# Second block's attention: sliding units mixed with selected ones, heads paired across key groups, block-diagonal compressed keys and values

## The reference

```
qn = rope(kvh(q_n, NSA_HEADS), t).reshape(B, S, NSA_KV, NSA_GROUP, HEAD_DIM)
k_c, k_s, k_w = (rope(kvh(z, NSA_KV), t) for z in (k_c, k_s, k_w))
ckv = jax.vmap(compress)(jnp.stack([k_c, v_c]), cmp_pos, cmp_w1, cmp_w2)   # 31 compressed blocks
o_cmp, p_cmp = compressed_attention(qn, ckv[0], ckv[1], t)
o_slc = selected_attention(qn, k_s, v_s, idx, t)       # 8 blocks of 64, all 8 are chosen: causal
o_win = banded_attention(qn, k_w, v_w, NSA_WINDOW, None)                   # window 512: causal
o_nsa = gates[..., 0:1] * o_cmp + gates[..., 1:2] * o_slc + gates[..., 2:3] * o_win
o_nsa = rms_norm(o_nsa.reshape(B, S, NSA_HEADS * HEAD_DIM), nsa_out_norm)
qw = rope(kvh(q_w, SWA_HEADS), t).reshape(B, S, SWA_KV, SWA_GROUP, HEAD_DIM)
o_swa = banded_attention(qw, kw, kvh(v_sw, SWA_KV), SWA_WINDOW, swa_sinks)  # window 128, with sinks
o_swa = rms_norm(o_swa.reshape(B, S, SWA_HEADS * HEAD_DIM), swa_out_norm)
h = h + rms_norm(jnp.concatenate([o_nsa, o_swa], axis=-1) @ w_out, attn_post_norm)
```

## Time and profile before

| | |
|---|---|
| median of 3 runs | 1889.32 us (1887.1 to 1889.44) |
| the profiled execution | 1890.05 us, its span 1888.2 us |
| TensorE busy | 1825.2 us (97%) |
| VectorE busy | 1332.4 us (71%) |
| ScalarE busy | 975.0 us (52%) |
| GpSimd busy | 190.9 us (10%) |
| HBM traffic | 81 GB/s over the span |

### The profile page before, as it was taken

The page is one execution under the profiler, slowest core; times in us unless marked ns, Lnnn a source line. Parts: engine busy times, 40 slices in busy tenths (PEclk is TensorE's granted clock), DMA queues, the critical chain, the costliest instruction groups (busy, mean ns, idle before and its releaser), DMA issues.

```text
span 1888.2 us, 26991 instructions
## 1 busy us (share of the span) xinstructions
PE 1825.2 (97%) x8975; PEld 1451.8 (77%) x8975; DVE 1332.4 (71%) x1885; ACT 975.0 (52%) x1550; POOL 190.9 (10%) x135
## 2 busy tenths in 40 slices
PE   6999999999999998999999999999898999999998
PEld 5775788888888875688888888887556678888887
DVE  6989777777655899867777755687675567777544
ACT  5468764444433458764444433576665554444322
POOL 0100120000133200020000033200021300000111
PEclk9999999999999999999999999999999999999999
DMA  6220233333233420133333233442000223332332
GB/s 168 71 80 1 65 92 100 93 96 97 77 99 99 109 73 23 33 91 99 90 100 100 72 97 99 109 143 79 12 1 12 78 78 100 91 98 86 89 95 76
DMA packets 285096, 154.46 MB, mean 82 GB/s; under 512 B 16949, under 2 KB 283095, under 8 KB 285015
## 3 DMA queue, kind: packets, MB, share of 16 engines
q1 hardware_dynamic: 284596, 153.26, 28.2%
q10 hardware_dynamic: 419, 0.17, 0.0%
HBM read 151.31 MB, written 2.10 MB: 81 GB/s over the span
## 4 chain that ended last, share of the span: by engine, by line
PE 79%; DVE 9%; issue 6%; ACT 6%; DMA 0%; DVEq 0%; SPq 0%; ACTq 0%
PE bank L575 24%; PE bank L576 24%; PE bank L577 24%; DVE cacc L1770 3%; PE bank L1019 1%; DVE nmax L1837 1%; PE bank L975 1%; PE bank L996 1%; ACT pr L1544 1%; DVE nmax L2071 1%; DVE w_lo L1630 1%; ACT w_hi L1177 1%; ACT pt L1560 1%; DMA x_in<-in_x 0%; PE bank L1091 0%
## 5 line engine op out<-in xcount | busy, mean ns | idle before, releaser
L575 PE MATMUL bank<-h_hi,w_hi 128*128 128x512 f32 x1448 | 571.7, 395 | 6.9 <-DVE w_lo L1630 6.7
L576 PE MATMUL bank<-h_lo,w_hi 128*128 128x512 f32 x1448 | 565.6, 391 | 0.0
L577 PE MATMUL bank<-h_hi,w_lo 128*128 128x512 f32 x1448 | 565.2, 390 | 0.0
L1177 ACT ACTIVATE w_hi<-raw 128x1024 fp32r<-128x1024 f32 (+3 forms) x314 | 312.0, 1000 | 488.2 <-PE bank L577 484.0
L1630 DVE TENSOR_TENSOR w_lo<-raw,w_hi 128x1024 fp32r<-128x1024 f32 (+3 forms) x314 | 375.4, 1201 | 230.9 <-ACT w_hi L1177 230.2
L575 PEld LDWEIGHTS bank<-h_hi,w_hi 128*128 128x128 f32 x1448 | 273.2, 189 | 69.7 <-issue 7.6
L576 PEld LDWEIGHTS bank<-h_lo,w_hi 128*128 128x128 f32 x1448 | 273.4, 189 | 57.8 <-issue 2.2
L577 PEld LDWEIGHTS bank<-h_hi,w_lo 128*128 128x128 f32 x1448 | 273.1, 189 | 57.3
L575 PE MATMUL bank<-a_hi,w_hi 128*128 128x512 f32 x528 | 206.1, 390 | 0.0
L577 PE MATMUL bank<-a_hi,w_lo 128*128 128x512 f32 x528 | 205.5, 389 | 0.0
L576 PE MATMUL bank<-a_lo,w_hi 128*128 128x512 f32 x528 | 205.4, 389 | 0.0
(11 more groups left out here) (317 smaller groups left out, 2258.4 us busy)
## 6 DMA issues: line engine op xcount, KB each, us to landing
raw<-in_w_up SPq DMA_DIRECT2D x132, 512.0 KB, 3.8
raw<-in_w_in SPq DMA_DIRECT2D x39, 512.0 KB, 4.0
raw<-in_w_down SPq DMA_DIRECT2D x48, 384.0 KB, 3.2
raw<-in_w_down SPq DMA_DIRECT2D x48, 320.0 KB, 3.0
raw<-in_w_o SPq DMA_DIRECT2D x16, 512.0 KB, 3.5
raw<-in_cmp_w SPq DMA_DIRECT2D x8, 512.0 KB, 3.9
raw<-in_w_out SPq DMA_DIRECT2D x8, 512.0 KB, 3.4
raw<-in_w_uq SPq DMA_DIRECT2D x8, 288.0 KB, 3.0
```

Of the source, the lines that this page charges most:

```text
L575: mm(o, wh, mh, start=start, stop=False)
L576: mm(o, wh, ml, start=False, stop=False)
L577: return mm(o, wl, mh, start=False, stop=stop)
L1177: last = A_(dst(w_hi), src(raw), ACT.Copy)
```

## The change

1. **Heads.** Pair c is now heads c and c+4, so that its two halves of the partitions belong to the two key groups. `k2` holds each key once (128 partitions x 512), and the rope's sum of ks, kw and kx is one addition of 128 partitions. The q slabs come in two DMAs of 64 columns each (256-byte runs), the output projection's slabs in two DMAs of 64 partitions; ScalarE's split waits for the second by semaphores of its own. Gates, sinks and norm gains are indexed to match.
2. **Compressed branch.** The 31 blocks are padded to 32, and `kcT` and `vcn` become block-diagonal over the two key groups (zeroed by VectorE ahead of the block; two copies each in place of one). `cmp_scores` makes 16 products of 128 rows and 64 columns, `cmp_turned` 4 groups of 4 turns of 64 columns, in k = 3 to 6 of slab t12, ScalarE 4 copies in place of 8. A windowed unit has one product of 64 rows and 128 columns for the compressed branch, in place of two of 31 rows and 64 columns.
3. **Order of the units.** After two NSA units the sliding units alternate with those of NSA pairs 0 and 1 (unit 2 is sliding, unit 3 selected, and so on), then come the last two sliding units; pairs 2 and 3 follow as before. All sliding chunks and the last windowed one gather in bank 7, the others in bank 6; a chunk's first values wait for the eviction of the chunk ahead in its bank. `yw` has a place of its own, 8 KB behind `ct_all`. The sink column is written only where the bank's unit before wasn't of the same sliding chunk: for 5 units in place of 8. The first sliding unit may start when its own query is roped.

```diff
-    [("qn", j, j * P) for j in range(4)] + [("qx", j, 1304 + j * P) for j in range(4)]
+    [("qn", j, j * HD2) for j in range(4)] + [("qx", j, 1304 + j * HD2) for j in range(4)]
...
-UNITS = nsa_units(0) + nsa_units(1) + [(SC_SWA, c, t) for c in range(PAIRS) for t in range(NT)] + nsa_units(2) + nsa_units(3)
-CHUNKS = [(SC_WIN, 0), (SC_WIN, 1)] + [(SC_SWA, c) for c in range(PAIRS)] + [(SC_WIN, 2), (SC_WIN, 3)]
+def mixed_units(lead):
+
+    nsa, swa = nsa_units(0) + nsa_units(1), [(SC_SWA, c, t) for c in range(PAIRS) for t in range(NT)]
+    pairs = [unit for both in zip(swa, nsa[lead:]) for unit in both]
+    return nsa[:lead] + pairs + swa[len(nsa) - lead:]
+
+
+UNITS = mixed_units(2) + nsa_units(2) + nsa_units(3)
+CHUNKS = [(b, c) for b, c, t in UNITS if t == NT - 1 and b != SC_SLC]
+O_BANK = {chunk: 7 if chunk[0] == SC_SWA or chunk == (SC_WIN, 3) else 6 for chunk in CHUNKS}
...
+def banked_ahead(u):
+
+    mine = chunk_of(u)
+    was = [chunk_of(n) for n in range(u) if O_BANK[chunk_of(n)] == O_BANK[mine] and chunk_of(n) != mine]
+    return [CHUNKS.index(was[-1]) + 1] if was else []
...
+def sink_new(u):
+
+    return UNITS[u][0] == SC_SWA and (u < 2 or UNITS[u - 2][:2] != UNITS[u][:2])
...
-                    c = T_ORDER[i][2]
-                    load(G2, p, slot(p, KD, P), d_in2[:, :, c:c + P])
+                    name, _, c = T_ORDER[i]
+                    if name[0] != "q":
+                        load(G2, p, slot(p, KD, P), d_in2[:, :, c:c + P])
+                        continue
+                    load(G2, p, slot(p, KD, P)[:, :, 0:HD2], d_in2[:, :, c:c + HD2])
+                    sp.dma_start(slot(p, KD, P)[:, :, HD2:P], d_in2[:, :, c + PAIRS * HD2:c + (PAIRS + 1) * HD2])\
+                        .then_inc(q2_ready[i - (len(T_ORDER) - 2 * PAIRS)], 16)
...
-                load(G2, S2_O + n, slot(S2_O + n, PAIRS, 2 * P), d_out2[:, k0:k0 + PAIRS, j * 2 * P:(j + 1) * 2 * P])
+                to = slot(S2_O + n, PAIRS, 2 * P)
+                of = A["w_out_2"][0].rearrange("(z e c p) n -> z e p c n", z=2, e=2, c=PAIRS)[k0 // PAIRS]
+                load(G2, S2_O + n, to[0:HD2, :, :], of[0, :, :, j * 2 * P:(j + 1) * 2 * P])
+                sp.dma_start(to[HD2:P, :, :], of[1, :, :, j * 2 * P:(j + 1) * 2 * P]).then_inc(o2_ready[n], 16)
...
                 for t in range(NT):
                     for c in range(PAIRS):
-                        for e in range(2):
-                            v0 = c // (PAIRS // KV2) * NC
-                            last = mm(C_B[e][:, (t * PAIRS + c) * NC:(t * PAIRS + c + 1) * NC], qn[half(e), c, t * P:(t + 1) * P],
-                                      kcT[half(e), v0:v0 + NC], start=True, stop=True)
...
+                        o = (t % 2 * PAIRS + c) * 2 * NCP
+                        last = mm(C_B[t // 2][:, o:o + 2 * NCP], qn[:, c, t * P:(t + 1) * P], kcT[:, :], start=True, stop=True)
...
             def turn_between(k):
-                for n in ((), (0,), (1,), (2,), (3,), (4,), (5,), (6, 7))[k]:
-                    cmp_turned(n)
+                if 3 <= k < 3 + NT:
+                    cmp_turned(k - 3)
...
-                    if b == SC_SWA and t < 2:
-                        last = mm(o[e][:, 2 * P:2 * P + 1], eye, sinks[:, 2 * c + e:2 * c + e + 1], start=True, stop=True)
+                    if sink_new(u):
+                        last = mm(o[e][:, 2 * P:2 * P + 1], eye, sinks[:, c + PAIRS * e:c + PAIRS * e + 1], start=True, stop=True)
...
-                if i == 1 and t == 0:
-                    pe.wait_ge(sw_done.sem, len(ROPED))
-                if t == 0 and i >= 2 and b != SC_WIN:
-                    pe.wait_ge(y_done.sem, y_done.at(N, i - 1))
-                    if i == 7:
+                if t == 0 and b != SC_WIN:
+                    if chunk_of(u) == (SC_SWA, 0):
+                        pe.wait_ge(sw_done.sem, len(ROPED))
+                    for n_ahead in banked_ahead(u):
+                        pe.wait_ge(y_done.sem, y_done.at(N, n_ahead))
+                    if chunk_of(u) == (SC_WIN, 3):
                         pe.wait_ge(rstd_done.sem, rstd_done.at(N, 3))
...
                 if b == SC_WIN:
-                    for e in range(2):
-                        last = mm(o[half(e), tok], vcn[0:NC, vc0:vc0 + HD2], ct_all[0:NC, c, t, e, :], start=False, stop=True)
+                    last = mm(o[:, tok], vcn[0:2 * NCP, :], ct_all[0:2 * NCP, t, c, :], start=False, stop=True)
...
                 else:
-                    outs = [(k2[kind][o * 64:(o + 1) * 64, hd, :], slice(hd * 64, (hd + 1) * 64))
-                            for hd in range(KV2) for o in range(2)]
-                for o, part in outs:
-                    last = v.tensor_tensor(o, tz[part, 2, :], tz[part, 3, :], ALU.add)
-                last.then_inc(rope_done.sem, 1)
+                    out = k2[kind][:, :]
+                v.tensor_tensor(out, tz[:, 2, :], tz[:, 3, :], ALU.add).then_inc(rope_done.sem, 1)
...
+            v.memset(kcT[:, :], 0.0).then_inc(flat_done.sem, 1)
+            v.memset(vcn[:, :], 0.0).then_inc(flat_done.sem, 1)
```

More of the change, by code:

```diff
@@ L394, in build @@
         vg_ready = [sem(f"vg_ready{i}") for i in range(NV)]
+        q2_ready = [sem(f"q2_ready{i}") for i in range(2 * PAIRS)]
+        o2_ready = [sem(f"o2_ready{i}") for i in range(KD)]
+        flat_done = tally("flat_done")
         xe_f, xe_h, xe_l = tally("xe_f"), tally("xe_h"), tally("xe_l")
@@ L886, in cmp_turn @@
                 for m in range(2):
-                    last = nc.tensor.transpose(bank[6 + t][:, m * 64:m * 64 + 2 * NC], hidc[0:2 * NC, t, m * P:(m + 1) * P],
-                                               const[0:2 * NC, K_EYE:K_EYE + 2 * NC])
+                    last = nc.tensor.transpose(bank[6 + t][:, m * 2 * NCP:(m + 1) * 2 * NCP], hidc[0:2 * NCP, t, m * P:(m + 1) * P],
+                                               const[0:2 * NCP, K_EYE:K_EYE + 2 * NCP])
                 last.then_inc(hid_t.sem, 1)
@@ L894, in cmp_keys @@
                 for m in range(2):
-                    last = mm(bank[4][:, 0:2 * NC], w2k[:, m, :], hid[:, m, :], start=m == 0, stop=m == 1)
+                    last = mm(bank[4][:, 0:2 * NCP], w2k[:, m, :], hid[:, m, :], start=m == 0, stop=m == 1)
                 last.then_inc(kv_mm.sem, 1)
@@ L900, in cmp_values @@
                 pe.wait_ge(sw_done.sem, 9)
[L901 to L904, removed]
+                for m in range(2):
+                    last = mm(bank[1][0:2 * NCP, 0:HD2], hid[:, 2 + m, :], w2v[:, m, :], start=m == 0, stop=m == 1)
                 last.then_inc(kv_mm.sem, 1)
@@ L975, in scores2 @@
                     mm(o[e][:, c0:c0 + n * P], q[half(e), c, t * P:(t + 1) * P],
-                       k2[k][half(e), c // (PAIRS // KV2), k0 * P:(k0 + n) * P], start=True, stop=False)
+                       k2[k][half(e), k0 * P:(k0 + n) * P], start=True, stop=False)
                 for e in range(2):
@@ L1173, in split @@
                     act.wait_ge(ukv_ready[n0 - S_UKV], (L + 1) * 16)
+                if isinstance(g, int) and g == G2 and S2_O <= n0 < S2_UP:
+                    act.wait_ge(o2_ready[n0 - S2_O], 16)
                 if n0 >= SPL:
@@ L1472, in hidden_out @@
             def hidden_out(t):
[L1473 removed]
+                A_(hidc[0:2 * NCP, t, :], bank[6 + t][0:2 * NCP, 0:CHID], ACT.Gelu_apprx_tanh).then_inc(hidc_done.sem, 1)
             def turned_out(t):
@@ L1495, in _ @@
                     act.wait_ge(kv_mm.sem, 2)
-                    A_(vcn[0:NC, :], bank[1][0:NC, 0:KV2 * HD2], ACT.Copy).then_inc(kv_done.sem, 1)
+                    for e in range(2):
+                        A_(vcn[e * NCP:(e + 1) * NCP, e * HD2:(e + 1) * HD2], bank[1][e * NCP:(e + 1) * NCP, 0:HD2],
+                           ACT.Copy).then_inc(kv_done.sem, 1)
                 if p < S2_O - 1:
@@ L1523, in _ @@
                     act.wait_ge(kv_mm.sem, 1)
-                    A_(kcT[:, :], bank[4][:, 0:2 * NC], ACT.Copy).then_inc(kv_done.sem, 1)
+                    act.wait_ge(flat_done.sem, 2)
+                    for e in range(2):
+                        A_(kcT[e * HD2:(e + 1) * HD2, e * NCP:(e + 1) * NCP], bank[4][e * HD2:(e + 1) * HD2, e * NCP:(e + 1) * NCP],
+                           ACT.Copy).then_inc(kv_done.sem, 1)
                 if (kind, i) == ("c", 7):
@@ L1970, in cmp_front @@
[L1970 to L1974 removed]
+                mask = const[:, K_CMP:K_CMP + NT * NCP].rearrange("p (t o c) -> p t o c", t=NT, o=1)
+                for z in range(2):
+                    dve.wait_ge(cs_mm.sem, z + 1)
+                    last = v.tensor_tensor(cs[:, z, :, :].rearrange("p (t h) n -> p t h n", t=2),
+                                           C_B[z][:, :].rearrange("p (t h n) -> p t h n", t=2, h=H2),
+                                           mask[:, 2 * z:2 * z + 2, :, :].to_broadcast([P, 2, H2, NCP]), ALU.add)
@@ L1975, in cmp_front @@
                 link(last)
-                for e in range(2):
```

(9 more changed lines are left out.)

123 lines of the change are left out of this document (64 added, 59 removed).

## The result

Before 1888.56 us (median, 1887.1 to 1889.44), after 1904.35 us (1900.73 to 1905.31): ratio 1.0081, 95% interval 1.0063 to 1.0098. The kernel became 0.8% slower, where 1887.0 (1881.5 to 1891.5) was forecast. The profiled execution after took 1904.71 us with a span of 1902.9, against 1890.05 and 1888.2.

A forecast was written before the change was run, and what follows sets the result against it. TensorE, busy nearly the whole span, was taken as the bound. Terms -1.0 -0.65 -0.8 -2.05 -0.8 +1.2 +1.7 = -2.4 from the profiled 1890.05, less 0.7 to the median, gave 1887.0 us, range 1881.5 to 1891.5.

The forecast's parts named there:

- Rival 3: Mixed part of the loop: clock stays at 1.2 GHz because steps leave idle pieces; over 1893.1, 20 us giving 1897; chance 0.06.
- Block-diagonal and rope: Ahead of the unit loop: key rope additions -1.0, compressed scores -0.65, clock behind them -0.8, turned compressed weights -2.05 us.
- its term: Compressed scores: half as many matmul records, limited by the wait for ScalarE's Gelu; -0.65 us, bounds 0 and -0.8.
- the next term: Slab behind the compressed scores: a shorter, denser burst may keep the clock; -0.8 us, bounds 0 to -1.6.
- Merged value product: Windowed units: one full-width product takes as long as two half-width ones side by side; 0, bounds 0 and -2.9 us.
- Sinks: Sink columns written for 5 units instead of 8, half the saving taken: -0.8 us, bounds 0 and -1.65.
- Mixing, start: Loop start: unit 2's values wait for ScalarE's copied(12), TensorE idle 4.5 us, low clock still losing 2.7; +1.2 us.
- rival 2: Loop start: clock falls already at the stand before unit 2, losing 2.7 us more, 1889.7; chance 0.16 together with rival 4.
- Mixing, after it: Mixed loop: TensorE idles at values behind three- and four-block units, 5.0 us lost against 3.3 before; +1.7 us.
- 1 (the mix fills gaps): Unit loop: step chains are shorter than assumed, so both mixing losses and 1.47 us idle vanish, 1882.6; chance 0.30.
- 4: Ahead of unit 0: block-diagonal gains don't reach the end, -2.05 and -0.8 gone, 1889.8; chance 0.16 together with rival 2.
- Transfers: q slabs and output projection weights in two DMAs each: hidden by 10 us or more before ScalarE's split; 0.

The follow-up runs named there:

- e2: Kernel before with an unused 32-byte tile ahead of the arena, moving it 128 bytes to the changed kernel's place: 1902.65 us, ratio 1.0074.
- e9: Kernel before with only a_hi and a_lo, the down projections' activations, moved 128 bytes on: 1899.90 us, ratio 1.0051 to the kernel before.
- e3: Changed kernel with the arena at its old place and the old order of units, banks and sink writes: 1880.96 us, ratio 0.9962 to the kernel before.
- e4: Changed kernel with the arena at its old place and the mix beginning after six NSA units, not two: 1884.61 us, ratio 0.9983 to the kernel before.
- e1: Changed kernel with the arena back at its old place (coef shares the place of cm): 1886.43 us, ratio 0.9991 to the kernel before.

## Why the prediction failed

**The step that failed** is a sentence of its first part: "the change touches nothing after it but the layout of the output projection's weights". By it the sum had no term outside the second block's attention, where 12.5 of the 14.7 us were lost. It was an argument from the code's instructions, and left memory out: the padding 31 to 32, costed at "0.1 to 0.3 us each beside waits", widened a tile ahead of the arena and displaced a_hi and a_lo. This edit carried +14 us by e2 (some 10 of them a_hi's and a_lo's by e9), none of it in the sum, the rivals or the list of what would show it wrong. Rival 3, the slower one, named another mechanism.

**Without the displacement** the changed kernel takes 1886.43, near the forecast of 1887.0. That is luck in part: the mix lost more than the sum had, and e3 gained more, in good part where nothing was changed.

**Block-diagonal and rope, -4.5 with -1.0, -0.65, -0.8 and -2.05: right in total.** From the block's `rstd` to the first reduction before took 108.27 us (1205.42 to 1313.69), after 103.68: -4.6. The wait for cw_lo is gone, and VectorE's 2.09 too. Within it sizes moved: `cmp_scores` took 3.76 us with half the records, so its term was nearer 0, and the clock behind it didn't fall at all (1.00), which is the bound of -1.6 of the next term. That these two errors nearly cancel is luck.

**e3, all but the mix: -7.2.** From the block's `rstd` to the next border behind the attention it takes 249.35 us against 254.86: 4.6 up to the first reduction and 1.0 in the attention's tail (64.7 against 65.8 from unit 32 on), 5.5 in all. The 1.0 may be no saved work: the clock in the tail is 1.00 in e3 and 0.97 before. The rest lies where nothing was changed: its profile has 1.3 less in layer 0's attention (133.0 against 134.4; all kernels lie between 133.0 and 134.7 there), with a mean clock of 0.99 against 0.97, 0.95 less before it and 1.1 less at the end. These are not explained by the change.

**Merged value product, 0: near.** It takes 0.42 (1344.06 to 1344.48), where the pair took 0.37: 0.05 more, 0.8 over 16 units, so that it loses a little and gains nothing. The Trainium skill (TensorEngine Tiling (Array Packing), Key Properties) has tiles that load and multiply in parallel, so that merging a pair gains nothing; the trace agrees, with 0.42 for two records against 0.37 for four. **Sinks, -0.8:** not told apart from the mix by any run, since e3 writes them for 8 units.

**Mixing, start +1.2: mis-sized.** The wait itself came as worked out, 4.43 for 4.5, and unit 2 starts 1.25 us behind the first reduction (1318.64 to 1319.89), as laid out. But the sum held the low clock to what it was before, 2.7 us lost; rival 2 had "as much again". It was at 0.50 for 15 us within 1323.5 to 1338.5 and 0.57 from 1345 to 1349. By e4, whose values don't wait for copied(12) and which has only 6.5 us at 0.50, both together are worth 4.7 in the profiles, and 1.8 by the medians of e1 and e4. **Mixing, after it +1.7: mis-sized too.** It was 2.7 by the profiles of e4 and e3, 3.7 by their medians. The sum had 0.2 and 0.3 us idle at the units with three blocks of keys and 0.7 and 0.8 at those with four, 2.0 a chunk. Measured in the second chunk of the changed kernel are 0.29 and 0.68 at three blocks, 0.90 at the first unit of four and hardly any at the second, and 0.28 to 0.55 at three steps of shorter units, where the sum had nothing: some 3.0 in all. Together the mix cost 7.4 in the profile and 5.5 by the medians, for 2.9, or for 2.1 with the sinks that these differences contain.

**Rivals.** 1 (the mix fills gaps) fell: e3 beats e1 by 5.5. 2 holds for the start of the profiled executions; by the mean clock it doesn't for those of e1 at 0.995. 3 needed the clock low through the whole mix and is wrong as put: from 1361 to 1407 it was 1.00, with 41.85 busy of 46 us. The Trainium skill (TensorE: Matmul & The Clock Gate, Part 4: PE-mode transpose) says that transposes don't count as busy in the same way; nearly a third of each unit is transposes, and this stretch at 1.00 gives no sign of it, though a mix with other matmuls is no test of transposes alone. 4 fell, by the 4.6. Transfers at 0 held: ScalarE's splits of the q slabs wait for no DMA in the trace after.

## What to carry to other kernels

Before calling a part of the kernel untouched, compare its tiles' addresses: a constant 16 bytes wider changed every matmul of the three down projections, and the distance of starts in the trace, not the duration, shows it. Keep the rows that stream through TensorE off the remainder that costs, or pin them. And where a stage hands over to one with shorter work per step, count what low clock a stall may bring, not the stall alone: here an order that put sliding steps beside long ones cost 2.7 us steadily by the profiles and more at the start. A part of a change that loses (the mix) also hid one that gains: without the mix the kernel takes 7.2 us less than before.

## What had not been expected of the hardware

- The pitch of a 512-column product of three-part fp32r operands at full clock depends on where its moving rows start in a partition: 0.2267 us at a remainder of 128 by 256 (bytes 138624 and 138880), 0.2333 at 0 (138752 and 139008). The runs by themselves show the step: moved by 0 or 256 bytes the tiles are fast, by 128 or 384 slow. Seen for a_hi and a_lo at all four places and for yq and uq; the rows here are 2048 bytes long. Why it is so is open.
- Low-clock stretches come and go in a part whose instructions are the same in all kernels: from its second `rstd` on, layer 1's attention takes 132.0 us with a clock of 1.00, or 134.2 to 134.8 with 0.97. One kernel's mean clock varies too, 0.988 to 0.995 among e1's executions. What decides isn't settled.
- 32 records of 128 rows and 64 columns took as long as 64 records of 64 rows and 31 columns: 3.76 us both, at a clock of 1.00.
